# Three 256-column matmuls per weight block into one accumulator, in a two-layer decoder trunk

## The reference, cut to what matters

```python
z, xbc, dt = _split(h @ w_in, [SSM_D_INNER, SSM_CONV_DIM, SSM_N_HEADS])    # 2048 x 10368
y.astype(h.dtype) @ w_out                                                  # 4096 x 2048
gate, up = _split(h @ w_gu, [FFN_HIDDEN, FFN_HIDDEN])                      # 2048 x 11264, twice
(jax.nn.silu(causal_dwconv(gate, conv_w, conv_b)) * up) @ w_down           # 5632 x 2048, twice
q, kc, vc, ks, vs, kw, vw, gates = _split(h @ w_in, ...)                   # 2048 x 5168
out @ w_out                                                                # 2048 x 2048
```

## Time and profile before

| What | Value |
|---|---|
| Time, median of 3 runs | 2688.85 us (2686.11 to 2694.59) |
| The profiled execution: span, first to last instruction | 2694.2 us |
| The profiled execution's own time | not given apart from its span |
| TensorE matmul busy | 2653.4 us, 98%, 15,411 matmuls |
| TensorE weight loads busy | 2309.0 us, 86%, 15,411 loads |
| VectorE busy | 1788.8 us, 66% |
| ScalarE busy | 1429.6 us, 53% |
| GpSimd busy | 198.0 us, 7% |
| DMA | 481.94 MB, mean 179 GB/s |

### The profile page before, as it was taken

How to read it: one execution, slowest core, us unless ns; L and a number is a source line. 1 busy time by engine, 2 the same in 40 slices (tenths; PEclk the granted TensorE clock), 3 DMA queues, 4 the chain that set the end, 5 groups by cost and what they waited for, 6 DMA issues and landing times. The chain is left out here.

```text
span 2694.2 us, 46463 instructions
## 1 busy us (share of the span) xinstructions
PE 2653.4 (98%) x15411; PEld 2309.0 (86%) x15411; DVE 1788.8 (66%) x2612; ACT 1429.6 (53%) x2210; POOL 198.0 (7%) x179
## 2 busy tenths in 40 slices
PE   7999999999999999999999999999999999999999
PEld 6888888888888888888888888888888888888888
DVE  7677777765677777775555765665677777775544
ACT  5676666654455555554444445654455555554343
POOL 0111111211200000000111000001300000000000
PEclk9999999999999999999999999998999999999999
DMA  5655555656555555556666555222555555556665
GB/s 185 214 192 190 193 187 187 193 168 188 177 187 187 185 185 185 185 185 186 186 187 190 184 184 191 94 94 80 182 183 186 184 185 185 186 186 181 189 189 167
DMA packets 135254, 481.94 MB, mean 179 GB/s; under 512 B 15104, under 2 KB 17152, under 8 KB 134160
## 3 DMA queue, kind: packets, MB, share of 16 engines
q1 hardware_dynamic: 132480, 467.72, 55.1%
q0 software_dynamic: 2336, 12.65, 1.4%
q10 hardware_dynamic: 368, 0.65, 0.1%
HBM read 478.80 MB, written 2.16 MB: 179 GB/s over the span
## 5 line engine op out<-in xcount | busy, mean ns | idle before, releaser
L683 PE MATMUL ps<-xn,w_hi 128*128 128x512 f32 x4768 | 1670.2, 399 | 12.1 <-DVE xn L996 9.4
L970 DVE TENSOR_TENSOR w_lo<-raw,w_hi 128x1024 fp32r<-128x1024 f32 x900 | 1102.2, 1226 | 743.8 <-ACT w_hi L350 742.5
L350 ACT ACTIVATE w_hi<-raw 128x1024 fp32r<-128x1024 f32 x900 | 938.2, 1043 | 915.1 <-PE ps L683 894.6
L682 PE MATMUL ps<-xn,w_lo 128*128 128x256 f32 x4470 | 1262.8, 283 | 6.2 <-DVE xn L1163 4.9
L683 PEld LDWEIGHTS ps<-xn,w_hi 128*128 128x128 f32 x4768 | 879.8, 188 | 208.9 <-DVE xn L996 9.8
L682 PEld LDWEIGHTS ps<-xn,w_lo 128*128 128x128 f32 x4470 | 846.1, 189 | 22.5 <-DVE xn L1163 5.9
L683 PE MATMUL ps<-hid,w_hi 128*128 128x512 f32 x1408 | 490.8, 396 | 0.0
L682 PE MATMUL ps<-hid,w_lo 128*128 128x256 f32 x1376 | 383.8, 279 | 0.0
L683 PEld LDWEIGHTS ps<-hid,w_hi 128*128 128x128 f32 x1408 | 262.1, 188 | 60.7
L682 PEld LDWEIGHTS ps<-hid,w_lo 128*128 128x128 f32 x1376 | 259.2, 188 | 1.5
L683 PE MATMUL ps<-y_ssm,w_hi 128*128 128x512 f32 x512 | 179.0, 397 | 0.0
(11 more groups left out here) (246 smaller groups left out, 1938.6 us busy)
## 6 DMA issues: line engine op xcount, KB each, us to landing
raw<-w_gu SPq DMA_DIRECT2D x352, 512.0 KB, 3.6
raw<-w_ssm_in SPq DMA_DIRECT2D x162, 512.0 KB, 3.6
raw<-w_down SPq DMA_DIRECT2D x128, 448.0 KB, 3.5
raw<-w_nsa_in SPq DMA_DIRECT2D x82, 512.0 KB, 3.6
raw<-w_ssm_out SPq DMA_DIRECT2D x64, 512.0 KB, 4.5
raw<-w_down SPq DMA_DIRECT2D x64, 512.0 KB, 3.6
raw<-w_nsa_out SPq DMA_DIRECT2D x32, 512.0 KB, 3.5
wcum<-cum_scratch POOLq DMA_DIRECT2D x8, 1024.0 KB, 7.2
```

The lines of the kernel that those rows point to most:

```text
L350: act.activation(w_hi[:, slot, 0:n * P], raw[:, slot, 0:n * P], ACT.Copy).then_inc(unit_rounded, 1)
L682: pe.matmul(acc[:, n:2 * n], lo, x[:, kb, 0:n], start=False, stop=False)
L683: mm = pe.matmul(acc[:, 0:2 * n], hi, x[:, kb, 0:2 * n], start=(kb == 0), stop=(kb == p.blocks - 1))
L970: TT(w_lo[:, slot, 0:n * P], raw[:, slot, 0:n * P], w_hi[:, slot, 0:n * P].bitcast(F32), ALU.subtract).then_inc(unit_split, 1)
```

## The change

The three products of a block now go to columns 0 to 255 of the bank. In `gemm_unit` TensorE waits for the rounding of the unit alone (`unit_rounded`), issues for each block two matmuls of 256 columns with w_hi (on the rounded part and on the rest), then waits for `unit_split`, and issues the unit's matmuls with w_lo. In `cmp_unit` the two matmuls of a block stay, in the same new order. `take_cross` is gone from ScalarE but for the four tiles of cmp. VectorE waits for `unit_used` itself; `take_tile` copies the accumulator out, or multiplies it by `rstd` in the one pass; the residual takes one addition. `cross` shrinks from 2x256 to 2x60 columns.

```diff
-        cross = sb("cross", [P, 2, T])
+        ccross = sb("ccross", [P, 2, KVG * NCMP])
...
+        def last_unit(p, k):
+
+            return p.unit0 + next(v for v in p.ends if p.ends[v] == k)
...
-            def take_cross(p, i, k, n=T):
-
-                t = p.tile0 + k + i * p.per_body
-                end = next(v for v in p.ends if p.ends[v] == k)
-                act.wait_ge(unit_used, p.unit0 + end + 1 + i * p.body)
-                if p.bank_age > 2:
-                    act.wait_ge(tile_out, t - 1)
-                act.activation(cross[:, (p.tile0 + k) % 2, 0:n], bank(p, k)[:, n:2 * n], ACT.Copy).then_inc(cross_copied, 1)
+            def take_cmp_cross(p, k):
+
+                act.wait_ge(unit_used, last_unit(p, k) + 1)
+                act.wait_ge(tile_out, p.tile0 + k - 1)
+                act.activation(ccross[:, k % 2], bank(p, k)[:, KVG * NCMP:2 * KVG * NCMP], ACT.Copy).then_inc(cmp_crossed, 1)
...
-                take_cross(p, 0, 0)
...
-                        take_cross(p, g, k)
...
-                        if v in p.ends:
-                            if n < 4 and p.ends[v]:
-                                weighted(n, i * p.per_body + (p.ends[v] - 1), p)
-                            take_cross(p, i, p.ends[v])
+                        if v in p.ends and n < 4 and p.ends[v]:
+                            weighted(n, i * p.per_body + (p.ends[v] - 1), p)
...
-                        if v == 1:
-                            take_cross(p_gu, j, 0)
...
+                slots = [(k0 + b, slice(b * P, (b + 1) * P)) for b in range(p.sizes[v])]
+                pe.wait_ge(unit_rounded, p.unit0 + v + 1 + i * p.body)
+                for kb, cols in slots:
+                    pe.matmul(acc[:, 0:n], w_hi[:, slot, cols], x[:, kb, 0:n], start=(kb == 0), stop=False)
+                    pe.matmul(acc[:, 0:n], w_hi[:, slot, cols], x[:, kb, n:2 * n], start=False, stop=False)
                 pe.wait_ge(unit_split, p.unit0 + v + 1 + i * p.body)
-                for b in range(p.sizes[v]):
-                    kb = k0 + b
-                    hi, lo = w_hi[:, slot, b * P:(b + 1) * P], w_lo[:, slot, b * P:(b + 1) * P]
-                    if kb:
-                        pe.matmul(acc[:, n:2 * n], lo, x[:, kb, 0:n], start=False, stop=False)
-                    mm = pe.matmul(acc[:, 0:2 * n], hi, x[:, kb, 0:2 * n], start=(kb == 0), stop=(kb == p.blocks - 1))
-                    if kb == 0:
-                        mm = pe.matmul(acc[:, n:2 * n], lo, x[:, kb, 0:n], start=False, stop=False)
+                for kb, cols in slots:
+                    mm = pe.matmul(acc[:, 0:n], w_lo[:, slot, cols], x[:, kb, 0:n], start=False, stop=(kb == p.blocks - 1))
                 mm.then_inc(unit_used, 1)
...
+                n = KVG * NCMP
+                slots = [((v % 4) * UNIT + b, slice(b * P, (b + 1) * P)) for b in range(UNIT)]
+                pe.wait_ge(unit_rounded, p.unit0 + v + 1)
+                for kb, cols in slots:
+                    wide = T if kb else T + n
+                    pe.matmul(acc[:, 0:wide], w_hi[:, slot, cols], x[:, kb * CMP_N:kb * CMP_N + wide], start=(kb == 0), stop=False)
                 pe.wait_ge(unit_split, p.unit0 + v + 1)
-                n = KVG * NCMP
-                for b in range(UNIT):
-                    kb = (v % 4) * UNIT + b
-                    hi, lo = w_hi[:, slot, b * P:(b + 1) * P], w_lo[:, slot, b * P:(b + 1) * P]
-                    xs = x[:, kb * CMP_N:kb * CMP_N + T]
-                    wide = T if kb else T + n
-                    if kb:
-                        pe.matmul(acc[:, n:n + T], lo, xs, start=False, stop=False)
-                    mm = pe.matmul(acc[:, 0:wide], hi, x[:, kb * CMP_N:kb * CMP_N + wide], start=(kb == 0), stop=(kb == p.blocks - 1))
-                    if kb == 0:
-                        mm = pe.matmul(acc[:, n:n + T], lo, xs, start=False, stop=False)
+                for kb, cols in slots:
+                    mm = pe.matmul(acc[:, n:n + T], w_lo[:, slot, cols], x[:, kb * CMP_N:kb * CMP_N + T], start=False, stop=(kb == p.blocks - 1))
                 mm.then_inc(unit_used, 1)
...
-            def tile_sum(p, i, k, dst, n=T):
-
-                dve.wait_ge(cross_copied, p.tile0 + k + 1 + i * p.per_body)
-                summed = TT(dst, bank(p, k)[:, 0:n], cross[:, (p.tile0 + k) % 2, 0:n], ALU.add)
+            def take_tile(p, i, k, dst):
+
+                dve.wait_ge(unit_used, last_unit(p, k) + 1 + i * p.body)
+                acc = bank(p, k)[:, 0:T]
                 if p.tile0 in SCALED:
-                    summed.then_inc(raw_sum, 1)
-                    dve.wait_ge(raw_sum, SCALED[p.tile0] + k + 1 + i * p.per_body)
-                    TT(dst, dst, rstd[:] if len(dst.shape) == 2 else rstd[:].unsqueeze(1), ALU.mult).then_inc(tile_out, 1)
+                    TT(dst, acc, rstd[:] if len(dst.shape) == 2 else rstd[:].unsqueeze(1), ALU.mult).then_inc(tile_out, 1)
                 else:
-                    summed.then_inc(tile_out, 1)
+                    dve.tensor_copy(dst, acc).then_inc(tile_out, 1)
+
+            def cmp_sum(p, k, dst):
+                dve.wait_ge(cmp_crossed, k + 1)
+                TT(dst, bank(p, k)[:, 0:KVG * NCMP], ccross[:, k % 2], ALU.add).then_inc(tile_out, 1)
...
-                dve.wait_ge(cross_copied, 1)
-                STT(h[0], ps[0][0:HEADS, 0:T], hc[:, 0:1], cross[0:HEADS, 0], ALU.add, ALU.add).then_inc(tile_out, 1)
+                dve.wait_ge(unit_used, last_unit(p, 0) + 1)
+                TS(h[0], ps[0][0:HEADS, 0:T], hc[:, 0:1], None, ALU.add).then_inc(tile_out, 1)
...
-                tile_sum(p, g, k, xpad[:, 3:3 + T])
+                take_tile(p, g, k, xpad[:, 3:3 + T])
...
-                            dve.wait_ge(cross_copied, p.tile0 + k + 1 + i * p.per_body)
-                            TT(row, row, cross[:, t], ALU.add).then_inc(resid_step, 1)
-                            dve.wait_ge(resid_step, RESID[p.tile0] + k + 1 + i * p.per_body)
+                            dve.wait_ge(unit_used, last_unit(p, k) + 1 + i * p.body)
                             TT(row, bank(p, k)[:, 0:T], row, ALU.add).then_inc(tile_out, 1)
```

More of the change, by code:

```diff
@@ L217, in trunk @@
         unit_used = sem("unit_used")
-        cross_copied = sem("cross_copied")
+        cmp_crossed = sem("cmp_crossed")
         tile_out = sem("tile_out")
@@ L223, in trunk @@
         ident_zero = sem("ident_zero")
-        resid_step = sem("resid_step")
         xsq_ready = sem("xsq_ready")
@@ L228, in trunk @@
         norm_y, xn_rounded, xn_ready = sem("norm_y"), sem("xn_rounded"), sem("xn_ready")
-        raw_sum = sem("raw_sum")
         out_stored = sem("out_stored")
@@ L275, in bodies @@
             body(p.n - 1, [unit_sizes[w] if w < len(unit_sizes) else 0 for w in range(end, end + p.body)])
[L277 to L280, removed]
+        SCALED = {ph[name].tile0 for name in ("gu0", "gates", "kvc", "kvs", "q", "gu1")}
+        def last_unit(p, k):
+            return p.unit0 + next(v for v in p.ends if p.ends[v] == k)
         NORM_OF = {ph["gu0"].tile0: 1, ph["gates"].tile0: 2, ph["gu1"].tile0: 3}
@@ L536, in body @@
                         if v == 3:
-                            take_cross(p_gu, j, 1)
                             act.wait_ge(h_formed, jj + 1)
@@ L548, in plain_tiles @@
             def plain_tiles(p, body_extra=None):
-                per = len(p.cuts)
                 def body(i, nxt):
@@ L555, in body @@
                             stream_std(2)
-                        if v % per == per - 1:
-                            take_cross(p, i, v // per)
                 bodies(act, p, body)
@@ L576, in kvs_body @@
                     round_unit(p.unit0 + RING + v, nxt[v], i, 4)
-                    if v % 2:
-                        take_cross(p, i, v // 2)
                     if is_body(i, 0) and v == 3:
@@ L591, in _ @@
                     k = v // 4
-                    take_cross(p, 0, k, KVG * NCMP)
+                    take_cmp_cross(p, k)
                     act.wait_ge(tile_out, p.tile0 + k + 1)
@@ L648, in q_body @@
                     round_unit(p.unit0 + RING + v, UNIT, g, p.body)
-                    if v % 2:
-                        take_cross(p, g, v // 2)
                     if not is_body(g, 0):
@@ L1145, in ssm_body @@
                             dve.wait_ge(yz_step, 2 * g)
-                        tile_sum(p, g, k, sz[:, k - 6])
+                        take_tile(p, g, k, sz[:, k - 6])
             dve.wait_ge(pad_set, 1)
@@ L1176, in body @@
                             k = p.ends[v]
-                            t = (p.tile0 + k) % 2
                             if n < 4 and k:
@@ L1189, in out_tiles @@
                     weighted_rest(n, D_TILES - 1)
-            RESID = {ph[a].tile0: D_TILES * n for n, a in enumerate(("ssm_out", "down0", "nsa_out", "down1"))}
             def ffn(l, p_gu, p_down):
@@ L1204, in body @@
                             dve.wait_ge(gtap, jj * 2)
```

(12 more changed lines are left out.)

## The result

The changed kernel takes 2728.57 us (2728.31 to 2728.72, 4 runs) against 2687.48 us for the kernel before (4 runs): ratio 1.0147, 95% interval 1.0133 to 1.0161. It is 41 us slower. The ratios of the experiments are against runs of the kernel before that were taken beside them, with medians of 2688.8 to 2689.7 us. The forecast was 2683 us and "the same". The time lies in the range given (2630 to 2735), on the side that had a chance of 0.25.

What follows compares the result with a forecast made beforehand. TensorE was taken as the bound, at 351.5 ns a block over 6,944 blocks. Part 1 at 0, Part 2 at 0 and Part 3 at -5.7 us, against the median of 2688.85, gave 2683 us, range 2630 to 2735.

Steps and rivals of the forecast that it cites:

- What bounds the kernel: Whole run: TensorE sets the pace, 98% busy, 351.5 ns a block, while ScalarE and VectorE wait on the full ring.
- Part 1: Each block: three narrow matmuls for a wide and a narrow one cost 351.5 ns again, 0 us (-87 to +59).
- The cmp phase: Nearest bound for a block: cmp's 256-column matmuls start every 117.6 ns, three make 352.9 ns, +10 us.
- Rival 2: Every block: the third load or a fixed start per matmul costs; at 120 ns each 2742 us; chance 0.20.
- The fixed cost: Every matmul: 2.5 ns whatever its width, +17 us, 2700 us with the tile ends; chance 0.05.
- Rival 1: Every block: equal matmuls run tighter, 2669 us at 349.5 ns a block, 2596 at 113 a matmul; faster case 0.37.
- Part 2: Within a unit: the new order and second wait, for unit_split, cost 0, as its semaphore is already raised.
- Rival 3: Unit middles: the second wait bites, 0.1 us at each of 900, +90 us, 2773 us; chance 0.05.
- Part 3: Tile ends: fewer copies and passes, -5.7 us: norm inputs -3.5, attention waits -1.3, last store -0.87.
- ScalarE's 1300 us: Sign of being right: ScalarE busy near 1300 us, with about 131 us of its copies gone.
- The wait for L1163: Sign of being right: TensorE's wait for the next norm's input falls to near 2.4 us from 4.9.
- 2 x 1134 w_hi matmuls in 400 us: Sign of being right: this count, +- 5, in a 400 us stretch, with starts 0.117 us apart in gu1.

Runs made afterwards that it cites:

- half_rest: Changed kernel with each block's second w_hi matmul cut from 256 to 128 columns, so three loads but 640 columns a block; 2662.0 us, a single run.
- after_shift: Changed kernel with 32 bytes of padding before and after xn, so xn, hid, y_ssm and o_nsa start 32 bytes off a multiple of 64; 2679.08 us, ratio 0.9959.
- after_pad: Changed kernel with padding behind ccross, so hid, y_ssm and o_nsa lie on a multiple of 64 bytes as in the kernel before; 2739.43 us, ratio 1.0186.
- before_shift: Kernel before with 32 bytes of padding per partition ahead of xn, so all moving tiles start 32 bytes off a multiple of 64; 2659.09 us, ratio 0.9888.
- mixed_after: Changed kernel with each block's w_lo matmul beside its two w_hi ones and one wait for unit_split at the unit's start; 2727.32 us, ratio 1.0137.
- after: The changed kernel itself, as measured without further edits; 2728.57 us, ratio 1.0147 against the kernel before.
- split_before: Kernel before with only the wide matmul issued as two of 256 columns, its halves, order and tile ends kept; 2746.44 us, ratio 1.0207.
- swap_align: Changed kernel with 32 bytes of padding ahead of xn: xn 32 bytes off a multiple of 64, hid, y_ssm and o_nsa on one; 2701.71 us, ratio 1.0044.
- w_shift: Changed kernel with w_hi and w_lo moved 32 bytes off a multiple of 64, xn on one, hid 32 off; 2698.56 us, ratio 1.0032.
- grouped_wide: Kernel before with its wide matmuls, but all w_hi matmuls of a unit first, then the wait for unit_split, then all w_lo ones; 2677.0 us, ratio 0.9942.
- grouped_shift: Kernel before grouped by unit (w_hi matmuls first, then w_lo), with 32 bytes of padding ahead of xn; 2683.45 us, ratio 0.998.

## Why the prediction was wrong, step by step

**What bounds the kernel** stood: TensorE's issue, block by block, with ScalarE and VectorE waiting on it.

**Part 1 is the step that failed**: "so I take 351.5 again: 0 us". It measured 359.7 and 355.5 ns, +46 us. Three things were wrong in it.
- The value was taken between bounds as if they were samples. They were different regimes. The lower one, 0.11 us between two narrow matmuls, is a pace that no long stream here holds. The upper one, 120 ns, is exactly where a stream of equal 256-column matmuls settles when weights and moving tile lie at the same place modulo 64 bytes.
- The cmp phase was called nearest, with the remark that its x steps by 120 columns "so it is not the same stream". That remark was the point. 120 columns are 480 bytes, so from block to block its rows stand at other distances from the weights, while the main stages have one distance throughout. That its 117.6 ns is a mean over these distances fits, and is not shown: no run changed cmp's steps, and its starts, 0.11 to 0.12 us apart before the change, show no plain turn between two paces.
- The load was priced at 0.11 us with nothing beside it, and that was set against 117.6 with the words "the cover is thin". In the stream a load costs 115.2 to 116.6 ns (half_rest), so there was next to no cover: three loads are 345.5 to 349.7 ns, where the two loads of before leave room in a block of 352.7. By the loads alone the 351.5 would have stood. The 360.0 is what the narrow stream costs with the tiles at the same place modulo 64, a condition that the prediction did not look at. With the tiles apart (after_shift) the changed kernel takes 2679 us, next to the forecast 2683. That is chance: the forecast was made for the addresses as they were, and at those of after_shift the kernel before is faster, too.

**Rival 2** came true, nearly to its number. It gave 120 ns each, 2742 us with the tile ends, and a decision point of 117.8 ns a matmul. With the addresses of before that is what after_pad measured, 2739.4. The mechanism was met by half: the third load does cost, but it gives 115 to 117 ns, and the rest comes with the addresses, which no rival named. That its price was exact is luck, since 120 was the mean of two distances rounded to 0.01 us, 0.11 and 0.13. The remaining 11 us to 2728.6 came from an effect that no part counted: the smaller `cross` moved hid, y_ssm and o_nsa.

**The fixed cost** of 2.5 ns a matmul (the Trainium skill, page "TensorE: Matmul & The Clock Gate", section "Back-to-back issue gap") would have given the right sign and 17 us. The one matmul more per block costs 7.0 ns in gu0 with the tiles aligned (352.7 to 359.7), and with them apart 2.2 ns in gu0 (before_shift 347.5, after_shift 349.7) and 6.2 in gu1 (before_shift 400 / 1151 = 347.5 there too, after_shift 353.7). One of these is near 2.5, and no single amount fits them all.

**Rival 1**, the tighter stream, did not occur in the changed kernel. A tighter stream exists at 116.6 ns, not at 113, and only with the tiles apart.

**Part 2** (the order and the second wait, 0) was right: mixed_after equals after. **Rival 3** falls with it.

**Part 3** (-5.7 us) was right in mechanism and near in size: 7.0 us by after_pad against split_before. Its terms were less good than their sum: the norm inputs gave 2.4 us for 3.5, the waits in the attention 2.1 (6.5 - 4.4) for 1.3.

Of the signs named: 22,355 matmuls and VectorE at 1670 us came in (1669.6). ScalarE's 1300 us did not (1331.3): the 131 us were the copies' whole durations, and ScalarE's instructions overlap in the trace. Their durations sum to 133 us less, while the busy time, which counts an overlap once, fell by 98. The wait for L1163 "near 2.4 us" did not come in (5.2), nor did 2 x 1134 w_hi matmuls in 400 us (2 x 1112). No hole before the first w_lo matmul was seen, as forecast. Starts every 0.120 us was one of the two paces named as signs of being wrong.

## What to carry to other kernels

Count loads as well as columns. At 256 columns of float32r the matmuls went no faster than their own weight loads do, 115 to 117 ns, so splitting a 512-column matmul adds a load that is barely hidden or not at all. Join the halves outside instead: here that costs 7 us, the split 57 (split_before) at the addresses of before, and some 27 with the tiles apart (20 + 7). Where two values bound a cost by regime, find out which regime the new stream is in rather than take the middle. And a change that resizes a buffer moves what is allocated behind it: compare at equal addresses before giving the difference to the edit, in both kernels.

## What the runs showed of the hardware that was not expected

- The pace of a stream of 256-column float32r matmuls depends on the distance of weight tile and moving tile: 120 ns where it is 0 modulo 64 bytes, 116.6 to 118.3 where it is 32. Moving either one does it (swap_align, w_shift). Within that range distance modulo 64 does not decide: hid took 118.3 in after and 116.7 in after_shift, 64 bytes farther on, and xn went from 116.6 in gu0 to 117.9 in gu1 of one run.
- Weight loads of 128 columns in a long stream start 115.2 (down0) to 116.6 ns (gu0) apart on average when one matmul in three is shortened to 128 columns (half_rest).
- Wide matmuls in a row go at 0.230 us with the distance 0 and at 0.234 with 32, against the trend of all the others (grouped_wide, grouped_shift).
- One allocation of 32 bytes ahead of xn makes the kernel before 1.1% faster (before_shift).
